# Four of the 24 modulation steps run in the last feed-forward instead of beside the first mixer's output projections

## The reference

```
c_act = silu(c)
mod = c_act @ w_ada + b_ada              # w_ada is 1024 x 6144
shift1, scale1, gate1, shift2, scale2, gate2 = split(mod, 6)
h = rms_norm(x, g_pre_mix) * (1 + scale1) + shift1
y = token_mixer(h, ...);          x = x + gate1 * rms_norm(y, g_post_mix)
h = rms_norm(x, g_pre_mlp) * (1 + scale2) + shift2
y = square(relu(h @ w_mlp_in)) @ w_mlp_out       # hidden width 4096
x = x + gate2 * rms_norm(y, g_post_mlp)
```

## Time and profile before

| | us |
|---|---|
| median of 3 runs (1121.47 to 1122.95) | 1121.82 |
| the profiled execution | 1122.09 |
| its span | 1120.3 |
| PE busy | 1058.2 (94%), 8193 matmuls |
| DVE busy | 796.0 (71%) |
| POOL busy | 492.8 (44%) |
| ACT busy | 479.8 (43%) |
| share of the chain that ended last: PE, DVE, ACT, DMA, POOL | 73%, 14%, 4%, 2%, 2% |
| TensorE's mean granted clock | 0.966 of full speed |

### The profile page before, as it was taken

One profiled execution on the slowest core, in us unless ns is written; L12 is line 12 of the kernel. 1 busy time (PEld: TensorE's weight loads), 2 busy tenths in 40 slices (PEclk: granted clock), 3 DMA queues, 4 the chain that ended last, 5 costly groups with the idle time before them and its releaser, 6 DMA issues.

```text
span 1120.3 us, 19883 instructions
## 1 busy us (share of the span) xinstructions
PE 1058.2 (94%) x8193; PEld 1019.3 (91%) x8193; DVE 796.0 (71%) x820; ACT 479.8 (43%) x527; POOL 492.8 (44%) x314
## 2 busy tenths in 40 slices
PE   8999999999989879999999999989799969999996
PEld 7989999998989779999999999978699959999995
DVE  6665666689776549887787759999969465555554
ACT  6333433566421335444334535553475443333332
POOL 2476675400076345566677899998500010000001
PEclk9999999999899989999999999998799979999998
DMA  8767686753402238767777355561225515555521
GB/s 250 274 227 259 206 283 208 230 164 113 124 28 76 76 113 288 241 201 249 230 251 230 113 152 170 147 205 53 76 79 186 155 48 174 187 187 185 180 85 38
DMA packets 165995, 188.81 MB, mean 169 GB/s; under 512 B 10575, under 2 KB 155549, under 8 KB 165821
## 3 DMA queue, kind: packets, MB, share of 16 engines
q1 hardware_dynamic: 165596, 186.14, 52.3%
q0 software_dynamic: 192, 1.88, 0.4%
q10 hardware_dynamic: 160, 0.14, 0.1%
HBM read 187.10 MB, written 1.05 MB: 168 GB/s over the span
## 4 chain that ended last, share of the span: by engine, by line
PE 73%; DVE 14%; issue 4%; ACT 4%; DMA 2%; POOL 2%; SPq 1%; DVEq 0%; POOLq 0%; ACTq 0%
PE ps L1773 44%; PE ps L1787 17%; PE ps L1949 4%; DVE ps L1515 3%; DVE wl L1150 3%; ACT wh L743 2%; PE ps L1801 1%; DMA raw<-in_ffn_w_in 1%; PE ps L1870 1%; PE ps L1933 1%; DMA ada_raw<-in_w_ada 1%; POOL ada_raw L618 1%; PE ps L1925 1%; PE ps L1818 1%; PE ps L2261 1%
## 5 line engine op out<-in xcount | busy, mean ns | idle before, releaser
L1773 PE MATMUL ps<-xh,wh 128*128 128x256 f32 x1272 | 370.1, 291 | 10.0 <-DVE xl L1707 3.3
L1773 PE MATMUL ps<-xl,wh 128*128 128x256 f32 x1272 | 364.8, 287 | 0.0
L1773 PE MATMUL ps<-xh,wl 128*128 128x256 f32 x1272 | 364.7, 287 | 0.0
L1155 DVE TENSOR_TENSOR wl<-raw,wh 128x2048 fp32r<-128x2048 f32 x78 | 214.8, 2753 | 83.8 <-ACT wh L749 83.7
L1773 PEld LDWEIGHTS ps<-xh,wh 128*128 128x128 f32 x1272 | 249.2, 196 | 16.1 <-issue 14.7
L1773 PEld LDWEIGHTS ps<-xl,wh 128*128 128x128 f32 x1272 | 249.4, 196 | 0.2
L1773 PEld LDWEIGHTS ps<-xh,wl 128*128 128x128 f32 x1272 | 249.1, 196 | 0.0
L749 ACT ACTIVATE wh<-raw 128x2048 fp32r<-128x2048 f32 x84 | 160.5, 1911 | 160.9 <-PE ps L1773 110.5
L1150 DVE TENSOR_TENSOR wl<-raw,wh 128x2048 fp32r<-128x2048 f32 (+1 forms) x74 | 183.3, 2485 | 59.2 <-ACT wh L743 55.1
L743 ACT ACTIVATE wh<-raw 128x2048 fp32r<-128x2048 f32 (+2 forms) x68 | 127.7, 1878 | 117.7 <-PE ps L1773 89.8
L1787 PE MATMUL ps<-fh,wh 128*128 128x256 f32 x560 | 157.9, 282 | 1.6 <-DVE fl L1216 1.6
(11 more groups left out here) (338 smaller groups left out, 1690.1 us busy)
## 6 DMA issues: line engine op xcount, KB each, us to landing
raw<-in_ffn_w_in SPq DMA_DIRECT2D x43, 1024.0 KB, 7.7
ada_raw<-in_w_ada SPq DMA_DIRECT2D x24, 1024.0 KB, 5.3
raw<-in_ffn_w_out SPq DMA_DIRECT2D x22, 1024.0 KB, 7.2
raw<-in_w_in SPq DMA_DIRECT2D x18, 1024.0 KB, 5.5
raw<-in_w_mlp_in SPq DMA_DIRECT2D x16, 1024.0 KB, 5.6
raw<-in_w_mlp_out SPq DMA_DIRECT2D x16, 1024.0 KB, 5.0
raw<-in_w_mix_in SPq DMA_DIRECT2D x14, 1024.0 KB, 5.5
raw<-in_w_mix_out SPq DMA_DIRECT2D x4, 1024.0 KB, 6.6
```

Source lines behind the costliest of these rows:

```text
L1155: dve.tensor_tensor(wl[:, s % SLOTS, :], raw[:, s % SLOTS, :], wh[:, s % SLOTS, :].bitcast(F32), ALU.subtract).then_inc(low_done, 1)
L1773: mm = pe.matmul(bank[:, m * T:(m + 1) * T], w[:, k, m * P:(m + 1) * P], r[:, k, :], start=(m == 0 and k == 0 and j == 0), stop=(k == KT - ...
```

## The change

The four steps that stood around the first mixer's output projections are taken out there. The second feed-forward now does steps 10 to 19 (`ADA_EARLY` = 20), and steps 20 to 23, which give `gate2`, stand in the loop of the last feed-forward (`ADA_MLP` = 4), one at the end of each round of six slabs. That loop on SP and on PE goes four rounds instead of five, and its fifth round is written out behind it. On DVE the bias and the gain of `gate2` are done in the last feed-forward, behind the step before last.

```diff
-ADA_MIX = 4
+ADA_MLP = 4
+ADA_EARLY = ADA_STEPS - ADA_MLP
 # SP, around ffn2's first slabs, and in its loop
-                    modulation(FF_STEPS - 1 + ADA_MIX)
+                    modulation(FF_STEPS - 1)
-                    modulation(i + (1 if name == "ffn1" else FF_STEPS + ADA_MIX))
+                    modulation(i + (1 if name == "ffn1" else FF_STEPS))
 # SP, mixer slabs and mix_out slabs
-                if n == 3:
-                    modulation(FF_STEPS - 1)
             for n in range(4):
                 wide(FIRST["mix_out"] + n, FIRST["mix_out"] + n, "w_mix_out", 256 * n)
-                if n:
-                    modulation(FF_STEPS - 1 + n)
 # SP, last feed-forward
-            with sp.Fori(0, (MLP_STEPS - 1) // SLOTS) as i:
+            with sp.Fori(0, ADA_MLP) as i:
                 for r in range(SLOTS):
 ...
                     deep(s + 1 + i * 6, s + 1, "w_mlp_out_2", i * 3 + r)
+                modulation(i + ADA_EARLY)
+            for k in range(ADA_MLP * SLOTS + 1, MLP_STEPS):
+                s = s0 + 2 * k - 1
+                wide(s, s, "w_mlp_in_2", 256 * k)
+                deep(s + 1, s + 1, "w_mlp_out_2", k - 1)
 # POOL
-            for n in range(ADA_MIX):
-                modulation(FF_STEPS - 1 + n)
-                modulation(i + (FF_STEPS - 1 + ADA_MIX))
+                modulation(i + (FF_STEPS - 1))
-            pool.wait_ge(*at("ada_taken", ADA_STEPS))
+            pool.wait_ge(*at("ada_taken", ADA_EARLY))
+            add_last("y", "x3_last")
+            with pool.Fori(0, ADA_MLP) as i:
+                modulation(i + ADA_EARLY)
+            add_last("z", "x4_last")
 # DVE, modulation_vectors: 40 columns, and no gain of gate2
-                dve.wait_ge(*at("ada_taken", ADA_STEPS))
+                dve.wait_ge(*at("ada_taken", ADA_EARLY))
-                dve.tensor_tensor(mods[:, 3, :], ada[:, 40:48], vecs("g_post_mlp_2"), ALU.mult)
 # DVE, last feed-forward
+            def last_gate():
+                g, r = VECS["b_ada_2"]
+                gate = slice(2 * ADA_EARLY, ADA_TILES)
+                dve.wait_ge(*at("ada_taken", ADA_STEPS))
+                st(dve.tensor_tensor(ada[:, gate], ps[7][:, gate], vec[:, g * P + r + 2 * ADA_EARLY:g * P + r + ADA_TILES], ALU.add))
+                st.sync()
+                g, r = VECS["g_post_mlp_2"]
+                st(dve.tensor_tensor(mods[:, 3, :], ada[:, gate], vec[:, g * P + r:g * P + r + KT], ALU.mult))
+                st.sync()
+                if k == MLP_STEPS - 2:
+                    last_gate()
 # PE
-                    modulate(i + (0 if name == "ffn1" else FF_STEPS - 1 + ADA_MIX))
+                    modulate(i + (0 if name == "ffn1" else FF_STEPS - 1))
-            modulate(FF_STEPS - 1)
 ...
-                if n:
-                    modulate(FF_STEPS - 1 + n)
-            with pe.Fori(0, (MLP_STEPS - 1) // SLOTS) as i:
+            with pe.Fori(0, ADA_MLP) as i:
                 for r in range(SLOTS):
 ...
                     deep(i * 6 + (s + 1), slab=s + 1)
+                modulate(i + ADA_EARLY)
+            for k in range(ADA_MLP * SLOTS + 1, MLP_STEPS):
+                s = s0 + 2 * k - 1
+                pe.wait_ge(*at("mlp_relu", k))
+                wide(s, ps[4], xh, xl)
+                pe.wait_ge(*at("mlp_fl", k))
+                deep(s + 1)
```

More of the change, by code:

```diff
@@ L721, in _, with add_last @@
                             ins.then_inc(S("long_conv"), 1)
-            for name, tag in (("y", "x3_last"), ("z", "x4_last")):
+            def add_last(name, tag):
                 pool.wait_ge(*at(name + "_gained", 4))
@@ L1184, in modulation_vectors @@
                 dve.tensor_tensor(final_sq, vecs("final_norm"), vecs("final_norm"), ALU.mult).then_inc(S("final_sq"), 1)
-                dve.wait_ge(*at("ada_taken", ADA_STEPS))
+                dve.wait_ge(*at("ada_taken", ADA_EARLY))
                 g, r = VECS["b_ada_2"]
-                st(dve.tensor_tensor(ada[:, :], ps[7][:, 0:ADA_TILES], vec[:, g * P + r:g * P + r + ADA_TILES], ALU.add))
+                n = 2 * ADA_EARLY
+                st(dve.tensor_tensor(ada[:, 0:n], ps[7][:, 0:n], vec[:, g * P + r:g * P + r + n], ALU.add))
                 st.sync()
```

## The result

| | before | after |
|---|---|---|
| median of the runs, us | 1121.82 (five runs, 1116.58 to 1123.2) | 1109.78 (five runs, 1107.78 to 1110.67) |
| ratio to before, 95% interval | | 0.9891 [0.9871, 0.991] |
| the profiled execution, us | 1122.09 | 1110.67 |
| its span, us | 1120.3 | 1108.9 |
| PE, DVE, POOL busy, us | 1058.2, 796.0, 492.8 | 1057.8, 820.4, 501.6 |

The change takes 12.0 us from the median and 11.4 from the profiled execution. I forecast 1107.5, with a range of 1104.3 to 1112.5. In what follows "the mixer's end" is the time from PE's first matmul behind the inversion (353.8 us before, 355.3 after) to its `tile_sum`, and "the last feed-forward" the time from the start of the first `mlp_in` slab in its loop (923.74 us before, 910.54 after) to the start of the `mlp_out` slab that stands behind all of them (1097.31 and 1085.88).

A forecast was written before the change was run, and what follows sets the result against it. The prediction took PE to bound the kernel, busy 94% of the span, with stops around the first mixer's end. Its terms, -0.9 - 14.86 + 1.36 = -14.4 us from 1122.09, gave 1107.7, stated as 1107.5; range 1104.3 to 1112.5.

The forecast's parts named there:

- Inversion: First mixer's inversion: without POOL's step 10 beside it, one level takes 5.50 us instead of 6.39, 0.9 us less.
- Split, stop and clock ahead of the second halves: Delta rule's half: split 2.29 us instead of 4.86, PE's 2.65 us stop gone, slab 5.75 us instead of 7.42.
- both slow pieces behind a stop: First mixer's end: two PE stretches at 1.2 GHz, costing about 1.7 us each, go with the stops before them.
- Queue and gate slab: First mixer's end: `ffn2`'s gate slab issued at 371.3 us, not 403.64; PE's 5.95 us stop goes; 14.86 us gained there.
- DVE's tail: Before `tile_sum`: DVE's residual, low parts and sum of squares, 6.10 us, become the late part, by 0.4 us.
- nothing else kept the projections slow: Rival at the first mixer's projections: DVE and ACT chains or PE's low clock cost 2 to 6 us; chance 0.16.
- Added steps: Last feed-forward: four `modulate` add 1.36 us; POOL's sum is ready at 970.2, eleven us before PE needs it.
- the ring: Rival in the last feed-forward: PE waits for POOL again, 7.7 us per step, 1138 in all; chance 0.03.
- DVE's slower splits: Last feed-forward: splits beside POOL longer by 3 us, `relu` late by about 2.1, hidden behind PE's deep slab.
- `last_gate` and the written-out round: Last feed-forward: `last_gate` under 0.6 us in DVE's idle time; fifth round 0, bounds -0.3 and +1; both cost nothing.
- The four `modulate`: PE in the last feed-forward: 0.34 us each, 1.36 in all, with bounds of 0.3 to 0.5 each.

The follow-up runs named there:

- e3: The kernel before, with PE taking each of the four modulation sums at the mixer's end one place earlier; median 1111.95 us, ratio 0.9917.
- e12_before: The kernel before, unchanged, profiled a third time; one run, 1116.9 us.
- e6: The changed kernel with steps 20 to 23 only as PE's matmuls, without their loads, POOL work and waits; median 1109.4 us, ratio 0.9895.
- e2: The changed kernel without steps 20 to 23, so gate2 isn't computed; median 1106.3 us, ratio 0.9845.

## Why the prediction was right

**Inversion.** Forecast -0.9, and a level is 5.50 instead of 6.39. Right against two executions of the kernel before; in the third the level took 6.02, so there only 0.5 us was to be won. Both lie within the bounds of 0 and 0.9.

**Split, stop and clock ahead of the second halves.** Right: 2.29, no stop, full speed behind, and one piece at 1.2 GHz in the first halves as counted. The Trainium skill (TensorE: Matmul & The Clock Gate, HAM oscillation — how this bites in real kernels) is borne out in that both slow pieces behind a stop went with it; the piece without a stop directly ahead of it stayed. The experiments agree: e3 keeps the first stop (2.3 us) and with it the 7.39 us behind it, and has the full clock from 413 to 425 us, where the second stop is gone. How the loss divides between a stop and the pieces around it changes: in e12_before the first halves ran slower (0.76 from 376 to 383 us), the stop was 0.9 and the slab behind it took 5.99.

**Queue and gate slab.** Forecast issue at 371.3, plus the 1.5 by which the inversion's end came later in this execution: 372.8, measured 372.86. Forecast was also that DVE's tail, not a load, would then be late; it is. The mixer's end became 14.8 us shorter, forecast 14.86. That the two agree within 0.1 is luck: against the other executions of the kernel before it is 14.1 and 13.7. In the rivals' terms, nothing else kept the projections slow.

**Added steps.** POOL's sum was forecast for 970.2 behind a load issued at about 952.4; the load went out at 950.85 and the sum was there at 970.9, nine us ahead of PE against the eleven forecast. The load took 7.3 us where 5.65 was counted, and POOL 12.8 where 12.1 was. The forecast called 12.1 the slowest step of the kernel before, and it was not: those that began at 430.73 and 524.97 us took 13.4 and 12.4. The cover was wide enough for all of this, and the ring was not rebuilt. The loop of `ffn2` kept its 17.5 us per round (440.96 to 458.53). DVE's slower splits (4.57 us) stayed hidden. Here the lockout that the Trainium skill describes (SBUF — State Buffer, Who interferes with whom) shows in the row and not in the time. `last_gate` and the written-out round cost nothing that e6 or e2 would show.

**The term that was mis-sized.** The four `modulate` were 1.36 in the sum and are 1.77. I read the gap between two pieces of the chain as their whole price, 0.34 each; the piece behind the gap is longer by 0.11 too. 0.44 lies within the bounds of 0.3 to 0.5. In `ffn2`'s loop the piece of the chain behind the gap holds two slabs, 11.47 us, and shows nothing of it; PE's timeline of the same place does, as shown above.

**The rest of the difference.** In the profiled execution the account is: +0.9 at the end of the first feed-forward, ahead of any change; +0.6 up to the inversion's end (-0.95 for the inversion, about +1.5 for the clock's place); -14.8; +0.1 between; +1.8. That is -11.4, against -14.4. Of the 3.0 missing, 0.4 is the term above and 2.4 lies in stretches that differ between executions of one kernel. How much of the 1.5 the change might cause is the open point above. The terms that the runs show for the change are -0.9, -14.8 and +1.8. The kernel before also has a shorter mixer's end in its two later executions (74.8 and 74.4), which puts that gain nearer 14.2; their sum is then -13.3. The medians of the three comparisons of the changed kernel with the one before give -12.0, -13.3 and -11.1, with intervals of two to four us each way; -13.3 lies in all three, and so does a gain smaller by one us. The forecast of 1107.5 was thus 2.3 us too low, well within its range of 1104.3 to 1112.5.

## What to carry to other kernels

A queue that issues loads in order passes a late wait on to every load behind it: look for transfers that were issued long after their buffer came free, and follow what stood ahead of them in the queue back to its engine. Work that lies "beside" a full PE is only free where no short chain of another engine feeds PE next; the same POOL step cost several us at the mixer's end and nothing in a loop in which PE stays the bound. When a small PE instruction is added to a dense loop, read its price from a whole round, with and without it, and not from the gap that it leaves.

## What the hardware did that I had not expected

- A wide slab right behind four one-column matmuls takes 5.86 us, and 5.75 behind a deep slab; the same in e6_pe_only, with no load and no POOL work near it.
- The same kernel needs 141.6 to 145.4 us for the stretch from the first feed-forward's end to the inversion's end (three executions of before), with the same instructions; all but about 0.5 us of it goes with the low granted clock at another place.
- Beside POOL's multiplication of 128x2048 a DVE subtraction of two SBUF tiles ends as if it had stood still until POOL was done: 2.15 us behind the multiplication, hardly less than the 2.29 that it needs alone, whenever it began: 388.50 against 386.35 in the kernel before, 601.95 against 599.81, and 964.22 against 962.06 after.
- The DVE subtraction takes 4.5 to 5.7 us there instead of 2.29, and yet POOL's own step in the last feed-forward took 12.8 us, little more than the 12.1 of the earlier trace rows and less than the 13.4 of its slowest step before.
